# Rounded products for keys, values and queries, and an earlier first output projection, in a streaming encoder step

## The reference, cut to what matters

```
h  = rmsnorm(x) * (1 + scale) + shift
cq, ckv, kr, ga, qb, kb, vb, qi, ki, wi, gb, ma, mb = split(h @ w_in)
q    = rmsnorm(cq) @ w_uq              # 8 heads of 64 + 32 (the 32 are rotated)
ckv  = rmsnorm(ckv); kr = rope(kr)
k, v = split(ckv @ w_ukv)              # 8 heads of 64 + 64
oa   = softmax(q k + rope(q) kr, chunk-causal) v
sel  = top_k(sum_h wi * relu(qi ki))   # per query; 128 of the prompt's keys
ob   = softmax(qb kb + bias, keys of sel only) vb
m    = sigmoid(ma) * ((oa * silu(ga)) @ w_oa) + sigmoid(mb) * ((ob * silu(gb)) @ w_ob)
x    = x + gate * (m @ w_out)
```

## Time and profile before

| | us |
|---|---|
| median of three runs | 1138.65 |
| profiled execution, its own time | 1136.84 |
| its span, first to last instruction | 1135.0 |
| mean granted clock of TensorE (1.0 is 2.4 GHz) | 0.972 |

### The profile page before, as it was taken

The page is one execution under the profiler, slowest core; times in us unless marked ns, Lnnn a source line. Parts: engine busy times, 40 slices in busy tenths (PEclk is TensorE's granted clock), DMA queues, the critical chain, the costliest instruction groups (busy, mean ns, idle before and its releaser), DMA issues.

```text
span 1135.0 us, 19935 instructions
## 1 busy us (share of the span) xinstructions
PE 1070.3 (94%) x7724; PEld 931.0 (82%) x7724; DVE 732.3 (65%) x1510; ACT 474.9 (42%) x1068; POOL 349.6 (31%) x208
## 2 busy tenths in 40 slices
PE   6999999999999999899989999999999999989995
PEld 3797986878788888799969789587887888879994
DVE  4538997646786777555672799955476323874655
ACT  4536455433444434414253554543354443451322
POOL 1346450220122222333334553302121222333340
PEclk9899999899999999899999999999899999999997
DMA  9581221201144445224314112121112121441322
GB/s 363 204 259 41 75 72 61 76 19 57 38 139 144 135 146 168 75 85 180 134 58 147 70 59 78 60 75 38 38 38 70 57 85 41 145 131 57 138 91 79
DMA packets 33774, 114.27 MB, mean 101 GB/s; under 512 B 4616, under 2 KB 5352, under 8 KB 31760
## 3 DMA queue, kind: packets, MB, share of 16 engines
q1 hardware_dynamic: 32352, 110.47, 29.2%
q10 hardware_dynamic: 1328, 2.53, 0.6%
HBM read 105.86 MB, written 7.12 MB: 100 GB/s over the span
## 4 chain that ended last, share of the span: by engine, by line
PE 82%; DVE 6%; ACT 5%; issue 3%; POOL 2%; DMA 2%; SPq 1%; POOLq 0%; DVEq 0%; ACTq 0%
PE pj L715 19%; PE pj L717 18%; PE pj L716 18%; PE ps L933 4%; PE po L1007 4%; PE turned L976 3%; PE pj L881 2%; PE ps L946 2%; DMA wide<-in_ada 2%; DVE squares L1587 1%; PE pj L855 1%; PE po L993 1%; POOL w_lo L1696 1%; PE pj L866 1%; PE ps L796 1%
## 5 line engine op out<-in xcount | busy, mean ns | idle before, releaser
L715 PE MATMUL pj<-h_hi,w_hi 128*128 128x272 f32 x1776 | 530.7, 299 | 17.4 <-POOL h_lo L1755 10.4
L717 PE MATMUL pj<-h_lo,w_hi 128*128 128x272 f32 x1776 | 518.0, 292 | 0.0
L716 PE MATMUL pj<-h_hi,w_lo 128*128 128x272 f32 x1776 | 515.7, 290 | 0.0
L1696 POOL TENSOR_TENSOR w_lo<-ring,w_hi 128x1024 fp32r<-128x1024 f32 x112 | 271.5, 2424 | 582.6 <-ACT w_hi L1095 582.6
L715 PEld LDWEIGHTS pj<-h_hi,w_hi 128*128 128x128 f32 x1776 | 339.6, 191 | 38.0 <-issue 28.3
L716 PEld LDWEIGHTS pj<-h_hi,w_lo 128*128 128x128 f32 x1776 | 340.1, 191 | 0.2
L717 PEld LDWEIGHTS pj<-h_lo,w_hi 128*128 128x128 f32 x1776 | 338.9, 191 | 0.0
L1095 ACT ACTIVATE w_hi<-ring 128x1024 fp32r<-128x1024 f32 x112 | 118.9, 1062 | 155.0 <-PE pj L717 139.0
L1587 DVE CUSTOM_DVE_ANT_0 squares<-ring,silu_c 128x1024 f32<-128x1024 f32 x64 | 84.6, 1322 | 1.4
L1544 DVE TENSOR_SCALAR probs<-probs,inv 128x128 f32<-128x128 f32 (+4 forms) x136 | 80.7, 593 | 4.8
L1318 ACT ACTIVATE wide<-pj 128x272 f32<-128x272 f32 x64 | 25.4, 397 | 114.5 <-PE pj L717 114.2
(11 more groups left out here) (285 smaller groups left out, 1342.1 us busy)
## 6 DMA issues: line engine op xcount, KB each, us to landing
ring<-in_wts SPq DMA_DIRECT2D x150, 512.0 KB, 3.5
wide<-in_xT SPq DMA_DIRECT2D x4, 1088.0 KB, 5.7
wide<-in_ada SPq DMA_DIRECT2D x3, 1024.0 KB, 20.2
ring<-in_wts SPq DMA_DIRECT2D x6, 384.0 KB, 3.1
x_between<-wide ACTq DMA_DIRECT2D x8, 272.0 KB, 2.0
wide<-x_between SPq DMA_DIRECT2D x2, 1088.0 KB, 6.3
bias_p<-in_ada SPq DMA_DIRECT2D x2, 1024.0 KB, 8.9
bias_p<-bias_rows SPq DMA_DIRECT2D x1, 2048.0 KB, 11.8
```

What stands on the lines that cost most here:

```text
L715: pe.matmul(out, hi, h_hi[:, k, half(b)], start=(k == first), stop=False)
L716: pe.matmul(out, lo, h_hi[:, k, half(b)], start=False, stop=False)
L717: return pe.matmul(out, hi, h_lo[:, k, half(b)], start=False, stop=(k == stop))
L1696: pool.tensor_tensor(w_lo[:, slot, :], ring[:, ring_slot[splits[n]], :], w_hi[:, slot, :].bitcast(F32), ALU.subtract).then_inc(s_wlo, 1)
```

## The change

Per layer:

- `uk`, `uv` and the three `uq` tiles (768 wide) join `SPLIT`: five more tiles pass ACT's `prepare` and POOL's `rest`, and the products become three rounded matmuls. The scaled latents are cut too: ACT copies `lat_hi` (two blocks of `ckv`, three of `cq`), DVE subtracts `lat_lo`.
- The squares are added on POOL (three additions), and PE makes one sum over channels per latent: the one of `ckv` within the stream of `cq`, the one of `cq` after the first block of `gb`. The roots move with them.
- DVE cuts `select(2)` in pieces of 8, 4 and 4 rounds, with the scaling of `ckv` after the first, the rest of `ckv` and the scaling of `cq` after the second, and the rest of `cq` after the third. Before the rotation only ten rounds of `select(3)` run, the other six in units 1 to 3, two in each; `select(4)` moves to units 4 to 20.
- ACT's eight copies of the rotated key into the heads move between the gates; the rounding of `cq` stands on ACT after the second of four outputs of `uk`. The swap of the rotation stands after the first block of `uqn` and no longer after the second.
- The tiles `gb` 2 and 3 move behind `ukt` in the order of loads, `prepare` and `rest`.
- The fillers are placed over 17 units from unit 18, so that the last is at unit 35. There ACT and DVE make the parts of the first half of `gate_a` and of three tiles of `gate_b`. In the pass 36, PE makes the first output projection `ya` (0, first half) ahead of the last values; the rests of the second half of `gate_a` are DVE's; PE waits for each tile by itself; `prepare` of `wo` 1 stands behind ACT's second half of `gate_a`.

The diff, cut to its core (buffers and semaphores left out):

```diff
-SPLIT = ("kx", "qi", "vb", "ga", "ckv", "cq", "gb", "qb", "kb", "ma", "mb", "wo", "wx")
+SPLIT = ("kx", "qi", "vb", "ga", "ckv", "cq", "gb", "qb", "kb", "ma", "mb", "wo", "wx",
+         "uk", "uv", "uq")
...
-    t += [("cq", n, P, 1024) for n in range(3)] + [("gb", n, P, 1024) for n in range(4)]
+    t += [("cq", n, P, 1024) for n in range(3)] + [("gb", n, P, 1024) for n in range(EARLY_GB)]
     t += [("uk", 0, P, 1024), ("uv", 0, P, 1024)] + [("uq", n, P, 768) for n in range(3)]
-    t += [("ukt", n, 64, 1024) for n in range(2)]
+    t += [("ukt", n, 64, 1024) for n in range(2)] + [("gb", n, P, 1024) for n in range(EARLY_GB, 4)]
...
-        u = FIRST_DSA + (i - dense) * FIRST_DSA // 31 if i >= dense else ...
+        u = FIRST_DSA + (i - dense) * (FIRST_DSA - 1) // 31 if i >= dense else ...
...
# PE
+                            if (kind, t, b) == ("cq", 1, 0):
+                                latent_sum(0, 1, squares[:, 0, :])
...
+                    if t == 0:
+                        latent_sum(1, 3, squares[:, 1, :])
...
+                pe.wait_ge(s_llo, past(s_llo) + 1)
+                pe.wait_ge(s_wlo, split_no["uk", 0] + 1)
                 for t in range(4):
                     out = bank(("uk", t, 0))
                     for c in range(2):
-                        last = pe.matmul(out[:, 0:TP], wt[:, c, P * t:P * t + P], ckv[:, c, 0:TP],
+                        pe.matmul(out[:, 0:TP], hi, lat_hi[c][:, 0:TP], start=(c == 0), stop=False)
+                        pe.matmul(out[:, 0:TP], lo, lat_hi[c][:, 0:TP], start=False, stop=False)
+                        last = pe.matmul(out[:, 0:TP], hi, lat_lo[c][:, 0:TP], start=False, stop=(c == 1))
...
+                    if u == NU:
+                        pe.wait_ge(s_wlo, split_no["wo", 0] + 1)
+                        attended("ya", 0, 0)
                     if u == last_ms + 2:
                         sample_values()
                     if u:
                         values(u - 1)
...
# ACT
+                    if t == 1:
+                        act.wait_ge(s_lno, 2)
+                        latents_hi(2, 3, cq)
+                prepare()
...
+                    if u == NU:
+                        output_hi(gate_a, 0, range(2), 1, s_gahi)
                     ...
-                    if u == NU:
+                    if u == NU - 1:
                         act.wait_ge(s_oev, uses - 1)
                         output_hi(gate_a, 0, range(4), 0, s_gahi)
                         output_hi(gate_b, 4, range(3), 0, s_gbhi)
...
-                output_hi(gate_a, 0, range(4), 1, s_gahi)
+                output_hi(gate_a, 0, range(2, 4), 1, s_gahi)
+                prepare()
...
# DVE
-                select(2, TOPK_P // 8)
-                select(3, 6, end=False)
-                ...
-                select(3, TOPK_P // 8 - 6)
+                select(2, 8, end=False)
+                latents_normed(0, 2, ckv, g_kv, 0)
+                select(2, 4, end=False)
+                latents_lo(0, 2, ckv, 0)
+                latents_normed(2, 3, cq, g_q, 1)
+                select(2, TOPK_P // 8 - 12)
+                latents_lo(2, 3, cq, 1)
+                select(3, 10, end=False)
...
                     else:
+                        output_lo(gate_a, 0, range(4), 1, s_gahi, s_galo)
+                    if u == NU - 1:
                         output_lo(gate_a, 0, range(4), 0, s_gahi, s_galo)
                         output_lo(gate_b, 4, range(3), 0, s_gbhi, s_gblo)
-                    if 1 <= u < 1 + TOPK_S // 8:
-                        select(4, 1, end=(u == TOPK_S // 8))
+                    if 1 <= u <= 3:
+                        select(3, 2, end=(u == 3))
+                    if 4 <= u < 4 + TOPK_S // 8:
+                        select(4, 1, end=(u == 3 + TOPK_S // 8))
...
# POOL
-                for t in range(4):
-                    pool.wait_ge(s_gahi, 4 + t + 1)
-                    pool.tensor_tensor(h_lo[:, t, half(1)], gate_a[:, t, half(1)], h_hi[:, t, half(1)].bitcast(F32),
-                                       ALU.subtract).then_inc(s_galo1, 1)
```

More of the change, by code:

```diff
@@ L806, in index_scores, with latent_sum @@
                         last.then_inc(s_isc, 1)
+                def latent_sum(n, added_to, total_of):
+                    pe.wait_ge(s_lsa, past(s_lsa) + added_to)
+                    for b in range(2):
+                        last = pe.matmul((ps, turned)[n][:, b, 0:HF], ones[:, :], total_of[:, half(b)], start=True, stop=True)
+                    last.then_inc(s_lst, 1)
                 places = index_places()
@@ L839, in layer_pe, with query @@
                         project(("gb", t, b))
-                pe.wait_ge(s_lno, 1)
-                loaded("uk", 0)
-                wt = w("uk", 0)[:, 0:1024].rearrange("p (c n) -> p c n", c=2)
+                    if t == 0:
+                        latent_sum(1, 3, squares[:, 1, :])
+                def query(job, tile, a, b):
+                    out = bank(job)
+                    for c in range(3):
+                        hi, lo = part_of(w_hi, tile)[:, 3 * a + c, :], part_of(w_lo, tile)[:, 3 * a + c, :]
+                        pe.matmul(out[:, 0:HF], hi, lat_hi[2 + c][:, half(b)], start=(c == 0), stop=False)
+                        pe.matmul(out[:, 0:HF], lo, lat_hi[2 + c][:, half(b)], start=False, stop=False)
+                        last = pe.matmul(out[:, 0:HF], hi, lat_lo[2 + c][:, half(b)], start=False, stop=(c == 2))
+                    last.then_inc(s_full, 1)
+                pe.wait_ge(s_llo, past(s_llo) + 1)
+                pe.wait_ge(s_wlo, split_no["uk", 0] + 1)
                 for t in range(4):
@@ L857, in layer_pe @@
                     last.then_inc(s_full, 1)
-                pe.wait_ge(s_lno, 2)
-                wt = w("uq", 0)[:, 0:768].rearrange("p (a c n) -> p a c n", a=2, c=3)
-                loaded("uq", 0)
+                pe.wait_ge(s_llo, past(s_llo) + 2)
+                pe.wait_ge(s_wlo, split_no["uq", 0] + 1)
                 for r in range(2):
                     for b in range(2):
[L864 to L867, removed]
+                        query(("uqr", r, b), ("uq", 0), r, b)
@@ L875, in layer_pe @@
                                           start=True, stop=True).then_inc(s_qsw, 1)
-                    loaded("uq", 1 + t // 2)
-                    wt = w("uq", 1 + t // 2)[:, 0:768].rearrange("p (a c n) -> p a c n", a=2, c=3)
+                    pe.wait_ge(s_wlo, split_no["uq", 1 + t // 2] + 1)
                     for b in range(2):
[L879 to L883, removed]
+                        query(("uqn", t, b), ("uq", 1 + t // 2), t % 2, b)
                 out = bank(("turn", 0, 0))
@@ L1742, in layer_pool @@
                 pool.wait_ge(s_gch, 1)
+                rest(5)
                 for t in range(EARLY_GB, 4):
```

164 lines of the change are left out of this document (99 added, 65 removed).

## The result

The changed kernel takes 1131.0 us (median of eight runs, 1128.6 to 1135.2) where the kernel before takes 1138.4 (eight runs). The ratio is 0.9943, interval 0.9928 to 0.9957: 6.5 us faster, 4.9 to 8.2. The forecast was 1131. Of all executions counted in this document one, of the run that kept PE busy before `uk`, took 3502.9 us and is left out of that run's ratio. The profiled execution took 1130.45 us, its span is 1128.7, 6.3 shorter than before, and the mean granted clock fell from 0.972 to 0.962.

A forecast was written before the change was run, and what follows sets the result against it. PE held 82% of the chain, but DVE would end last before attention. Savings of 0.7 and 0.4 us there, 3.8 and 2.9 in the tails, sum to 7.8: 1129.0 profiled, 1131 median; range 1120 to 1142.

The forecast's parts named there:

- the stretch: From the latents to attention: attention starts earlier by 0.7 us in layer 0 and 0.4 in layer 1.
- the tails: End of each layer's attention units to output tile 0: 3.8 us saved in layer 0, 2.9 in layer 1.
- the clock in the tails: Sign of being right: granted clock 1.00 in either tail, with no wait of PE over 2 us.
- PE's products: Keys, values and queries before attention: rounded products take 24.4 us for 30.2; with fewer sums, 8.6 us less work.
- The wait before `uk`: PE waits 4.2 us for the keys' `w_lo` on POOL, so its saving only moves into a wait.
- rival C: Both locks fall and the clock drops before `uk`, some 2.4 us a layer: 1139 us in all; chance 0.18.
- the second lock: Before attention, the `w_lo` of `gb` 3 blocks DVE's fourth rotation set: another 2.4 us, counted half.
- my plan of ACT: Before attention, ACT's rounding of `cq` behind two outputs of `uk` ends at 173.45, when DVE's `lo(cq)` can start.
- Rival D: Clock falls before `uk` and stays at half: +14 us a layer, about 1160 us in all; chance 0.12.
- DVE's chain: Selection and rotation on DVE end last before attention, which starts at 201.4, 203.95 or 206.3 by locks falling.
- That cover: Units 1 to 3: PE's 3.0 us filler hides 1.5 us more selection in each; cost 0, otherwise 4.4 a layer.
- the lock of `wo` 1's `w_lo`: In the tail it can hold a rest of `gate_a`: tile 0 ends at 476.7 instead of 475.5; taken half way.

The follow-up runs named there:

- the stretch alone: The changed kernel with the old tail, so only the latents and the three rounded products are new: ratio 0.9987 to the kernel before.
- `wo` 1 early: The changed kernel with ACT's prepare of the second output tile right behind the last filler's output at unit 35: ratio 0.9924 to the kernel before.
- `wo` 1 late: The changed kernel with ACT's prepare of the second output tile put back behind all roundings of the gated outputs: ratio 0.9922 to the kernel before.

## Why the prediction was right

**The direction and the size of the sum** hold: 7.8 us forecast on the profiled execution, 6.4 measured there and 7.4 between the medians. Two terms missed in opposite directions, and by about as much: in the two profiles the stretch gave 3.3 for 1.1, the tails 4.7 for 6.7. That they cancel, and the median comes out at 1131.0, is luck. Of the signs named for being right one failed (the clock in the tails), and of those named for being wrong two came: a granted clock under 0.9 from `uk` on, and a tail in which `ya`'s second product waits for its rests (0.43 and then 1.80).

**PE's products.** Right in what mattered: they are shorter and don't count. (The 1.52 us of the earlier trace rows wasn't PE's only wait in the stretch before: three of 0.60 to 0.67 us stood there too; none enters the sum.) Keys, values and queries take PE 24.7 us at full clock (48 x 0.233 and 108 x 0.125) for the 24.4 forecast; the 512-column matmul is 0.233, near the upper bound of 0.236 and not the 0.2255 taken.

**The wait before `uk`.** Forecast 4.2, measured 4.25; `uk` at 166.1 for 166.8. "PE only moves its saving into a wait" is what the run with fp32 keys confirms: with 1.3 us more work (16 x 0.429 for 24 x 0.233), `uk` ended 4 us earlier. What I set aside as rival C is there: the clock fell to 0.50 behind that wait and stayed until 172.0 (in layer 1 from 714.7, 0.7 us into `uk`, to 718.1). Its price, 2 us a layer by the run that kept PE busy, lies inside the measured stretch, which nevertheless came out better than forecast, because the second lock, which I had counted at half (1.2 us a layer), didn't fall, and because my plan of ACT was late: with the clock up, the rests of `cq` began at 172.3 (174.68 less the 2.36 by which that run is behind at the latent sum), not at 173.45. Rival D, half clock to the end of `uqn`, did not come: 5.9 us of it from the start of `uk` in layer 0 and 3.4 in layer 1, under the 10 from which it would have decided.

**DVE's chain.** Planned and measured: rests of `cq` at 173.45 and 174.71, rotation through at 203.9 and 204.5, attention at 203.95 (one lock) and 204.56. The locks are shown by both signs: 3.99 with the `w_lo` inside, 1.77 without; 3.88 and 1.78 in layer 1. That the second one didn't fall was luck, by 0.22 and 0.04 us: of the eight layers with this stretch it fell in two (layer 1 of the stretch alone and of `wo` 1 early). In those two the absorbed queries had run in 3.75 us, in the other six in 4.04 to 5.88. `gb` 3 is loaded when the first of their tiles is used up, so it seems that slow absorbed queries held its `w_lo` back; no run tested that.

**Units.** No cost of the two rounds more in units 1 to 3: the lead of 1.7 us at the start is the same in units 1 to 3. That cover held.

**The tail** is where the forecast was too good: 13.3 us from `turn` to the end of tile 0 in layer 0, 11.5 without a lock and 12.7 with it forecast. The term that was mis-sized is the lock of `wo` 1's `w_lo`, 1.2 us taken at half. It fell whole in both layers (3.67 for 1.50) and cost 2.0, by two tails at clock 1.00: with `wo` 1 late, where the rests take 1.50, tile 0 ended 11.0 us behind `turn`; in layer 0 of the run with fp32 keys, where they take 3.67, the second tile began, with no wait before it, at 13.0. The clock is the smaller part. "In the new order no wait of PE there is over 2 us" came true, but it was taken to mean that the clock holds: three waits came close together (0.87, 0.43, 1.80), and the clock fell to 0.54 all the same (the tail's window after). Its price is 0.3: in layer 1 of the run with fp32 keys, where the clock fell too, the second tile began at 13.4.

## What to carry to other kernels

Before shortening an engine's work in a stretch, find which engine ends the stretch last; 8.6 us a layer taken from TensorE here bought at most a quarter of that, while two lines moved on ScalarE bought 5 us in the whole kernel. A product that needs prepared operands isn't shorter if its preparation ends later than the longer product would. And a subtraction on GpSimd has to be placed like a lock: in the places tried here but one it blocked a VectorE instruction with two SBUF operands, and in that one, behind the rotation, PE waited 0.88 us for its result.

## What the runs showed of the hardware that was not expected

The clock fell behind a wait of the same length in some places and executions and not in others. Before the sample's values PE waits 1.58 or 1.59 us in every layer of both kernels; after it the clock was 0.50 in layer 0 and 1.00 in layer 1 of the changed kernel (windows at 244 and 790 above), the other way round in the kernel before (the same stretch there, layer 0 and 1):

```profile
245.00:249.00 4.00, 4.00 (x31) 3.60 (x32) 1.30 (x5) 1.18 (x5) 0.00 (x0) 1.00 0.00 0
793.00:797.00 4.00, 4.00 (x16) 3.27 (x16) 0.00 (x0) 0.00 (x0) 0.00 (x0) 0.50 0.00 0
```

From these values to PE's next wait of about a microsecond it is 38.4 us in layer 0 of the changed kernel and 35.3 before; 36.8 in layer 1, where the clock fell later on (806.8 to 813.7), and 38.3 before. So this piece alone differs by +3.1 and -1.4 us between the two profiles, where all the units together differ by +1.9 and -1.3 in the table. In the tail the waits of 0.87, 0.43 and 1.80 were followed by half clock in both layers of the changed kernel, and in the run with fp32 keys by full clock in layer 0 and half clock in layer 1. Between two groups of eight transposes around the sample's values (at 231.12 and 278.38 in layer 0 of the changed kernel) the profiles range from 42.5 to 47.3 us with the same work; single runs of one kernel lie up to 10 us apart, and differences under 2 us had to be read from a stretch within a trace.

The absorbed queries, 32 records of 32 columns, took between 3.75 and 6.07 us; in the changed kernel the clock was at 0.50 from 200 to 205 us, with PE busy for three quarters of that time. And an instruction of DVE that multiplies two operands and sums (L1638, `adaptive`) is blocked by `w_lo` as an addition is: 3.25 us for 1.22.
